# Moving the first logits and half of the first output item past the two ends of sparse attention, with new homes for their probabilities

## The reference

```python
(u_h, u_b, u_c, z_a, q, k, v, qi, ki, wi, z_b, g_a, g_b) = _split_proj(h @ w_in)
q = _rms(q, q_norm); k = _rms(k, k_norm)
branch_a = (u_b * conv_out) * silu(z_a)
branch_b = attend(q, qi, wi, k, v, ki) * silu(z_b)
merged = sigmoid(g_a) * (branch_a @ w_pa) + sigmoid(g_b) * (branch_b @ w_pb)
y = x + gate * (merged @ w_out)
# attend: index scores -> top 256 allowed keys -> softmax(q k^T / sqrt(128)) v, 8 heads of 128, 2 kv heads
```

## Time and profile before

| | us |
|---|---|
| three runs | 3180.42, 3181.79, 3182.03 (median 3181.79) |
| the profiled execution | 3181.93 |
| its span, first to last instruction | 3180.1 |
| PE busy in the span | 3108.9 |
| DVE, ACT, POOL busy | 1932.5, 1202.5, 904.0 |
| mean granted TensorE clock | 0.995 of full |

### The profile page before, as it was taken

One profiled execution on the slowest core, in us unless ns is written; L12 is line 12 of the kernel. 1 busy time (PEld: TensorE's weight loads), 2 busy tenths in 40 slices (PEclk: granted clock), 3 DMA queues, 4 the chain that ended last, 5 costly groups with the idle time before them and its releaser, 6 DMA issues.

```text
span 3180.1 us, 47676 instructions
## 1 busy us (share of the span) xinstructions
PE 3108.9 (98%) x18495; PEld 2703.0 (85%) x18495; DVE 1932.5 (61%) x3876; ACT 1202.5 (38%) x2104; POOL 904.0 (28%) x829
## 2 busy tenths in 40 slices
PE   7999999989999999999999999999999999999999
PEld 6999999957987888888888888889888788889987
DVE  5443696044634994048357999268527688878861
ACT  3445332355324221145234221155326444226551
POOL 2345775454520332023200331111310133111110
PEclk9999999999999999999999999999999999999999
DMA  8765688775974555731754556610563455660026
GB/s 296 260 209 196 212 273 298 256 270 164 308 245 159 192 198 197 236 125 62 268 173 148 204 191 209 234 63 13 215 223 117 158 196 195 214 230 13 11 77 230
DMA packets 266530, 599.32 MB, mean 188 GB/s; under 512 B 17693, under 2 KB 177623, under 8 KB 216130
## 3 DMA queue, kind: packets, MB, share of 16 engines
q1 hardware_dynamic: 255796, 558.38, 51.2%
q0 software_dynamic: 10368, 37.75, 3.5%
q10 hardware_dynamic: 142, 0.13, 0.0%
HBM read 453.65 MB, written 142.57 MB: 187 GB/s over the span
## 4 chain that ended last, share of the span: by engine, by line
PE 90%; DVE 5%; DMA 2%; ACT 1%; issue 1%; POOL 1%; SPq 0%; ACTq 0%; DVEq 0%; POOLq 0%
PE ps L1240 83%; PE ps L1245 6%; DVE SC L2055 1%; DVE RS L2014 1%; DVE PTL L2275 1%; DMA MW<-in_w_mod 1%; DMA GB<-gb_scratch 0%; DMA WR<-in_w_proj_b 0%; DVE LP L2292 0%; DVE XN L1888 0%; ACT PTH L1110 0%; DVE MG L2373 0%; DVE OB L2303 0%; POOL WLH L2482 0%; DVE T L2372 0%
## 5 line engine op out<-in xcount | busy, mean ns | idle before, releaser
L1240 PE MATMUL ps<-HTH,WLH 128*128 128x512 f32 x3504 | 1128.6, 391 | 0.0
L1240 PEld LDWEIGHTS ps<-HTH,WLH 128*128 128x128 f32 x3504 | 658.4, 188 | 139.6 <-issue 5.0
L1240 PE MATMUL ps<-HTL,WLH 128*128 128x512 f32 x1752 | 682.5, 390 | 0.0
L2127 DVE TENSOR_SCALAR_CACHE_REDUCE JUNK<-SC,SMALL 128x1920 bf16<-128x1920 f32 (+5 forms) x364 | 514.2, 1413 | 14.6 <-POOL sSC L2568 1.7
L1240 PE MATMUL ps<-H,WLH 128*128 128x288 f32 x3504 | 479.8, 297 | 4.5 <-POOL H L2541 2.2
L1240 PEld LDWEIGHTS ps<-H,WLH 128*128 128x128 f32 x3504 | 470.3, 190 | 6.5 <-issue 2.7
L2292 DVE CUSTOM_DVE_ANT_0 LP<-ps,SC,RQ 128x512 f32<-128x512 f32 (+3 forms) x320 | 202.5, 666 | 306.3 <-PE ps L1240 305.6
L1240 PEld LDWEIGHTS ps<-HTL,WLH 128*128 128x128 f32 x1752 | 329.4, 188 | 65.1
L948 ACT ACTIVATE T<-ps 128x512 f32<-128x512 f32 x192 | 115.0, 599 | 646.8 <-PE ps L1240 642.2
L2482 POOL TENSOR_TENSOR WLH<-WR,WLH 128x1024 fp32r<-128x1024 f32 x97 | 235.5, 2428 | 308.5 <-ACT WLH L770 308.4
L2055 DVE SCALAR_TENSOR_TENSOR SC<-T,WI,SC 128x512 f32<-128x512 f32 (+3 forms) x266 | 179.1, 698 | 120.6 <-ACT T L882 120.2
(11 more groups left out here) (369 smaller groups left out, 5191.0 us busy)
## 6 DMA issues: line engine op xcount, KB each, us to landing
WLH<-w_scratch SPq DMA_DIRECT2D x291, 1024.0 KB, 4.8
w_scratch<-WLH SPq DMA_DIRECT2D x97, 1024.0 KB, 5.6
WR<-in_w_in SPq DMA_DIRECT2D x73, 512.0 KB, 4.4
MW<-in_w_mod SPq DMA_DIRECT2D x6, 2048.0 KB, 16.3
q_scratch<-QO SPq DMA_DIRECT2D x32, 256.0 KB, 5.6
ma_scratch<-T SPq DMA_DIRECT2D x32, 256.0 KB, 5.6
gb_scratch<-GB SPq DMA_DIRECT2D x32, 256.0 KB, 5.6
QU<-q_scratch SPq DMA_DIRECT2D x64, 128.0 KB, 2.2
```

The source lines that it names most:

```text
L1240: return pe.matmul(out, lhsT, rhs, start=start, stop=stop, **more)
L2127: ins_ = dve.tensor_scalar(JUNK[0:n, 0:row.shape[1]], row, MID[0:n, c:c + 1], 0.0, ALU.is_ge, ALU.add, accum_out=CNT[0:n, c:c + 1])
```

## The change

In the tiles 1 to 3 PE issues the logits of unit 0 ahead of the last `zb` item instead of behind it, and four of the eight steps of the first `pb` item ahead of the values of the last unit. Since the activations and the early BBH and BBL are then in use, the probabilities of unit 0 and of the last two units get places of their own, and DG and TB move. ACT takes the exponentials of unit 0 before it evacuates the last `zb` item. POOL makes both parts of slices 0 to 3 of BB. `whole_keys` is cut in two: the first half goes ahead of unit 14's diagonals, the second behind the last `attn_low`. The text of the SP block is the same.

```diff
+    LP_FIRST = at("LP_FIRST", [P, 2, SEQ], F32, rM)
+    LP_LAST = [at(f"LP_LAST{i}", [P, 2, SEQ - TILE], F32, rS + 12288 * i) for i in range(2)]
+    LP_LAST3 = [at("LP_LAST30", [P, 2, SEQ], F32, rS), at("LP_LAST31", [P, 2, SEQ], F32, rKH)]
...
-    DG = at("DG", [P, 4, P], F32R, rKH + 6144)
-    TB = [at(f"TB{i}", [P, 256], F32, rKL + 6144 + 1024 * i) for i in range(2)]
+    DG = at("DG", [P, 4, P], F32R, rGT)
+    TB = [PFX[:, 0:256], PFX[:, 256:512]]
...
+    EARLY = range(4)
# ACT
-                if u < len(UNITS):
+                if 0 < u < len(UNITS):
                     exponentials(t, u)
...
-                    attn_high(t, range(KC - 2))
+                    attn_high(t, range(len(EARLY), KC - 2))
...
-                if i == len(PROJ_B) - 1:
+                if i == len(PROJ_B) - 2:
                     query_high(t, 0)
                     query_high(t, 1)
+                if t and i == len(PROJ_B) - 1:
+                    exponentials(t, 0)
# PE
             for i in range(len(PROJ_B)):
+                if t and i == len(PROJ_B) - 1:
+                    head_logits(t, 0)
                 products(j)
...
-                head_logits(t, 0)
                 for u in range(len(UNITS)):
...
+                    if u == len(UNITS) - 1:
+                        products(j, steps=EARLY)
                     head_values(t, u)
...
+                elif f == 0:
+                    products(j, steps=range(len(EARLY), KC))
# DVE
             dve.wait_ge(*gate_mul.at(t, KC - 1, "P"))
+            mask_logits(t, 0)
             dve.wait_ge(*evac.at(... len(PROJ_B) - 1 ...))
-            mask_logits(t, 0)
...
-            attn_low(t, 1)
             finish(t, len(UNITS) - 1)
...
-                for k in (3, 5, 7):
+                for k in (5, 7):
                     attn_low(t, k)
# POOL
+        def attn_halves(t, k):
+            if k == 0:
+                pool.wait_ge(*p_t.at(t, len(UNITS) - 3, unit_groups(t, len(UNITS) - 3) - 1))
+            pool.wait_ge(*attn_z.at(t, (BLOCKS - 1, k // 2)))
+            link(pool.tensor_copy(BBH[:, k, :], BB[:, k, :]))
+            pool.tensor_tensor(BBL[:, k, :], BB[:, k, :], BBH[:, k, :].bitcast(F32), ALU.subtract)...
...
+                    if u == len(UNITS) - 2:
+                        attn_halves(t, 0)
+                        attn_halves(t, 1)
                     diagonals(t, u)
-                    if u == len(UNITS) - 2 and t + 1 < TILES:
-                        whole_keys(t)
-            if t:
-                for k in (0, 2, 4, 6):
+                    if u == len(UNITS) - 2:
+                        attn_halves(t, 2)
+                        attn_halves(t, 3)
+                    if u == len(UNITS) - 3 and t + 1 < TILES:
+                        whole_keys(t, 0)
+                for k in (4, 6):
                     attn_low(t, k)
+                if t + 1 < TILES:
+                    whole_keys(t, 1)
```

More of the change, by code:

```diff
@@ L84, in parts, with product_bank @@
     return ("P", "S") if t == 0 else ("P",)
-PRODUCTS = [(j, p) for j, (t, n, f) in enumerate(GEMMS) for p in parts(t)]
-PBANK = {jp: i % 4 for i, jp in enumerate(PRODUCTS)}
+FIRST_BANK = {1: 2}
+def product_bank(j):
+    t, i = divmod(j, WEIGHTS)
+    before_out = len(PROJ_A) + len(PROJ_B)
+    if t == 0:
+        return 2 * (i % 2)
+    if i == before_out - 1:
+        return 3
+    return (i - before_out if i >= before_out else i + FIRST_BANK.get(t, 0)) % 4
+PBANK = {(j, "P"): product_bank(j) for j in range(len(GEMMS))}
 class Signal:
@@ L146, in program, with probabilities @@
     HTL = at("HTL", [P, KC, TILE], F32R, rH + 16384)
-    LP = [at("LP0", [P, 2, 2, TILE], F32, rM)] + [at("LP", [P, 2, 2, SEQ], F32, rH)] * (TILES - 1)
+    LP0, LPU = at("LP0", [P, 2, 2, TILE], F32, rM), at("LP", [P, 2, 2, SEQ], F32, rH)
+    LP_FIRST = at("LP_FIRST", [P, 2, SEQ], F32, rM)
+    LP_LAST = [at(f"LP_LAST{i}", [P, 2, SEQ - TILE], F32, rS + 12288 * i) for i in range(2)]
+    LP_LAST3 = [at("LP_LAST30", [P, 2, SEQ], F32, rS), at("LP_LAST31", [P, 2, SEQ], F32, rKH)]
+    def probabilities(t, u):
+        if t == 0:
+            return LP0[:, u % 2]
+        if u == 0:
+            return LP_FIRST
+        if u >= len(UNITS) - 2:
+            return (LP_LAST3 if t == TILES - 1 else LP_LAST)[len(UNITS) - 1 - u]
+        return LPU[:, u % 2]
     BBH = at("BBH", [P, KC, TILE], F32R, rH)
@@ L441, in program @@
     bb_high, bb_low_pool, bb_low_dve = signal("bb_high"), signal("bb_low_pool"), signal("bb_low_dve")
-    bb_ready_at = lambda t, k, p: (bb_low_dve if p == "P" and k % 2 else bb_low_pool).at(t, k if p == "P" else 0, p)
+    EARLY = range(4)
+    on_dve = lambda t, k, p: p == "P" and k % 2 == 1 and not (t and k in EARLY)
+    bb_ready_at = lambda t, k, p: (bb_low_dve if on_dve(t, k, p) else bb_low_pool).at(t, k if p == "P" else 0, p)
     merged, mg_ready = signal("merged"), signal("mg_ready")
@@ L1095, in exponentials @@
                 act.wait_ge(*row_max.at(t, u, hh))
-                row = LP[t][:, u % 2, hh, 0:w]
+                row = probabilities(t, u)[:, hh, 0:w]
                 act.activation(row, row, ACT.Exp, bias=NM[:, u % 2, hh:hh + 1],
@@ L2291, in mask_logits @@
                     dve.wait_ge(*qk.at(t, u, hh, c))
-                    ins_ = dve.tensor_tensor_reduce(LP[t][:, u % 2, hh, c:c + n], ps[bank("qk", t, u, hh, c)][:, 0:n],
+                    ins_ = dve.tensor_tensor_reduce(probabilities(t, u)[:, hh, c:c + n], ps[bank("qk", t, u, hh, c)][:, 0:n],
                                                     scores(t)[:, blk, c:c + n], RQ[:, blk, 2 * pr + hh:2 * pr + hh + 1],
@@ L2315, in finish @@
                 left = halves(ps[acc_bank(t, u)][:, 0:256])
-                link(dve.tensor_tensor(halves(TB[u % 2][:, :]), right, gate, ALU.mult))
-                right, gate = left, halves(TB[u % 2][:, :])
+                link(dve.tensor_tensor(halves(TB[u % 2]), right, gate, ALU.mult))
+                right, gate = left, halves(TB[u % 2])
             dve.tensor_tensor(BBT[t][:, 2 * pr:2 * pr + 2, blk * P:(blk + 1) * P], right, gate, ALU.mult
@@ L2530, in both_attentions @@
                 if s == len(UNITS) + LEAD - 1:
-                    whole_keys(0)
+                    whole_keys(0, 0)
+                    whole_keys(0, 1)
             attn_low(0, 0)
```

28 lines of the change are left out of this document (13 added, 15 removed).

## The result

The changed kernel takes 3204.98 us (median of 4 runs, 3200.40 to 3206.37), the kernel before 3181.91 in the same session: a ratio of 1.0069, 95% interval 1.0055 to 1.0082. It is slower, as forecast, but by 23 us between the medians where 7 were forecast, and outside the range. The profiled execution took 3200.40, 18.5 us more than that of before. PE's busy time hardly moved, so the time is waits and low clock.

A forecast was written before the change was run, and what follows sets the result against it. PE is busy 3108.9 of 3180.1 us, so only its waits and low clock count. Tiles 1 to 3 give +5.45, +1.65, -1.35, together +5.75; with 1.5 for clock on 3181.9, 3189 us, range 3177.5 to 3195.

The forecast's parts named there:

- Head, tile 1: Tile 1, last `zb` item to first values: 2.25 us longer; bounds 1.0 shorter to 2.6 longer.
- it lands at P + 5.3 or a little later: Tile 1 head: QU, behind a 1 MB weight load, lands no sooner than before; PE starts at P + 6.3.
- P: The moment at which PE leaves the last `zb` item; 1389.57 in tile 1 of the old kernel.
- Heads, tiles 2 and 3: Start of attention: +0.6 us in tile 2 (0 to +1.0), +0.4 in tile 3 (0 to +0.8).
- Tail, tile 1: Tile 1, last values to `pb` item 1: item 1 starts about 0.5 us later (-0.2 to +1.1).
- Tails, tiles 2 and 3: Early half fills ACT waits: -1.85 us in tile 2, -1.75 in tile 3 (-2.8 to -1.2).
- The second half of KT: Its late writing delays GB and `pb` item 3's weights: item 3 +3.2 us in tile 1, +1.05 in tile 2.
- GB is issued at 2260.3, lands at 2263.0, and the weights at 2271.9: Tile 2: kept 8.9 us from GB's landing to the weights' landing; item 3 starts then, +1.05 us.
- Clock: PE stands about 3 us in three new places; one fall likelier than three, counted as 1.5 us.
- rival D: Clock falls at each new gap, three more falls of 1.5 us, item 3 at its upper bounds: 3194; chance 0.15.
- B: Loads not in the way, QU and item 3's weights arrive in time: -4.1 us, 3178; chance 0.18.
- C: Beside B, POOL has slices 2 and 3 in time in tile 1: -9 to -12 us, about 3171; chance 0.07.

The follow-up runs named there:

- the second experiment: The changed kernel with unit 2's queries loaded ahead of the load that waits for the last `zb` item, tiles 1 to 3; 3193.98 us, ratio 1.0039.
- the last experiment: Against both edits, PE does no step of the first `pb` item ahead of the last values; 3181.66 us, ratio 0.9996 to the kernel before.
- the tail in another order: Against both edits, DVE finishes unit 14 ahead of the last probabilities, ACT casts slices 2 to 5, DVE and POOL share subtractions; 3187.67 us, ratio 1.0009.
- both edits: The changed kernel with KT's second half ahead of the last unit's diagonals and unit 2's queries loaded earlier; 3182.66 us, ratio 1.0003.

## Why the prediction was wrong in size

**Head, tile 1: +2.25 forecast, +4.2 measured.** The step "it lands at P + 5.3 or a little later" failed. QU was issued at P + 0.56 in place of P + 2.44 and landed at P + 7.2: 1.9 us sooner out, 1.9 later in. The load of 1 MB landed after 4.8 us as in the earlier trace rows, and QU only 2.2 us behind that, the median of all its loads. The bytes agree: 363 GB/s moved between 1398 and 1399, 137 between 1399 and 1400 (one QU is 128 KB) and 7 in the next microsecond, so QU went behind the weights. In the earlier trace rows the two had landed almost together; why they did there and not here is open. The mechanism (ACT held by QU, PE by ACT's first PTH) is shown by moving that one issue: P + 3.2. Of the bounds, -1.0 held (with QU in time the head is 0.8 shorter than before, 3.2 + 2.25 against 6.28); "up to 2.6 longer" did not, because it left out that a load behind a 1 MB load may pay that load's 4.8 and its own 2.2 in full.

**Heads, tiles 2 and 3: +0.6 and +0.4; +0.7 and +0.3.** Right. So was the table load: the one at 1403.11 takes 1.28 us and the exponential starts at 1404.40, right behind it. That differs from the Trainium skill, "ScalarE: Activation LUTs" (What ACT_TABLE_LOAD costs), by whose drain it would have been 2.66. With QU in time, as in the second experiment, these two heads come out within 0.2 us of the kernel before, so even then moving the logits gains only in tile 1.

**Tail, tile 1: +0.5.** The +1.9 in the table is the low clock behind the head (2.0, from the runs without that wait) and -0.1. But the kernel before has 111.0 with a low clock in it and 109.9 in its second profile without one, so the tail itself is about 1 us longer: 0.5 more than forecast. POOL's four slices break it up as the prediction says, but less (a wait of 0.9 where 2.4 was worked out inside the early half), and the second half of the item then waits 2.0 behind the last values.

**Tails, tiles 2 and 3: -1.85 and -1.75; -1.9 and -1.55 at the end of item 1.** Right in size by luck, wrong in reason. "The early half (12 x 0.23 = 2.7 us) fills the waits" is what PE does, and the last experiment shows it to be worth nothing. What is left to explain the gain is POOL's earlier slices.

**The second half of KT: item 3 starts 2.7 later in tile 1 and 2.9 in tile 2, counted from item 0's end; 4.5 and 7.9 measured.** This is the term that failed most. SP's issue of GB was forecast well: 6.3 and 7.3 us behind the last values, 6.9 and 7.5 measured. The failing step is "GB is issued at 2260.3, lands at 2263.0, and the weights at 2271.9". I took the 8.9 us from GB's landing to the weights' landing as fixed and let GB land in 2.7. But GB's 7.1 in the old kernel was part of the same stream. Counted from GB's issue to the weights, the old kernel has 2254.1 to 2270.2, 16.1 us, and the new one 2275.8 to 2291.6, 15.8. With 16.1 in place of 11.6 the forecast for tile 2 would have been 4.5 higher, of the 5.0 that were missing.

That agreement is partly luck. In tile 1 the same count is 15.5 us in the old kernel (1499.37 to 1514.9) and 13.4 in the new one (1516.75 to 1530.19), so it would have been 2.1 too long there. The old kernel had 1 MB of weights (tile 1) or 2 MB (tile 2) issued just ahead of GB, which had landed in the new one; the new stream in tile 2 in turn began slowly, with 152 and 195 GB/s from 2276 to 2280 where the old one had 400 or more from 2256 on. What set that pace was not found. Tile 1's own forecast chain was 12.2 us (1508.3 to 1520.5; with the 11.6 of tile 2 it would end at 1519.9), 1.2 short of the 13.4, and GB came out 0.6 later than forecast: together the 1.8 that were missing there.

XN's 2 MB are a large part of the stream (4.5 of the wait of 7.1 by experiment), and the old kernel moved them while PE had two items to do. The Trainium skill, "DMA: Bandwidth & Descriptors" (Queues, rings and completion order), has descriptors consumed in ring order; the experiments that move QU and XN in SP's queue agree with it. The order alone gives no size: in the new kernel's window from 2285 on PE stands still while the transfers run at 423 GB/s, so there it waits for bytes.

**Clock: one fall of 1.5 forecast; three of 2.0, 1.45 and 1.7.** Item 3 of tile 1 takes 6.9 and that of tile 2 7.2 instead of 5.44. "One fall is likelier than three" was read off single waits of 2.4 in the earlier trace rows; the new waits are 4 to 7 us. Even the row behind it was chance: the same 2.40 had a low clock behind it when the kernel before was profiled again. Filling two of the three new waits with matmuls took the fall away. This is rival D's mechanism, which I gave 0.15. Its 3194 was too low because it kept the forecast's waits.

The rivals B and C (the loads are not in the way) are out: two edits that let those loads go earlier, and take no work from any engine, give back 22 us. C's own terms also come to no more than -9.5, not to -12 (-4.1, 3.7 of waits and gaps, 1.2 to 1.7 of clock). The 4.6 us between the profiled execution and the median of the result stay open. The three other executions have a granted clock of 0.992 against 0.995, and no trace of them was taken.

## What to carry to other kernels

When an edit delays the release of a DMA queue, don't shorten a landing time that was read under load and then add the rest of the old chain to it. Count from the first delayed issue to the last landing that matters, with all bytes between them and those still in flight ahead of them; such a count was good to 0.3 us in tile 2 and 2.1 too long in tile 1, so give it a range of that width. Work hoisted ahead of a long item gains only what the next operand's transfer allows, so look first whether that transfer can be issued ahead of the same item. Price a wait of PE with the clock behind it: in these kernels a wait of 4 to 7 us cost 1.5 to 2 us more.

## What the runs showed of the hardware

- Every wait of PE between 4.1 and 7.2 us in tiles 1 to 3, ten in six traces, was followed by a granted clock of 0.50 to 0.7. Of the waits of 1.9 to 2.9 us some were (2.4 and 2.6 with XN late, a 2.0 with the second half of KT earlier, a 2.1 with the tail in another order) and some not (2.0 in most traces, 2.4 with both edits, 2.9 in tile 3 with the tail in another order). The 2.4 of tile 3 went both ways in two executions of the same program.
- A wait of 1.2 us in the middle of tile 3, in all twelve traces, had a low clock within about 3 us behind it in four of them.
- The same 48 matmuls of 288 columns take 6.24 us in one execution and 6.40 in eleven others over a whole stretch, at a granted clock of 1.00 in all. What sets it was not found.
- A 128 KB load issued 0.4 to 0.5 us behind a 1 MB load on the same queue landed after 4.7 us in one place and after 6.7 in another, in the same execution; the median of all 64 is 2.2.
